# Attention's value products in three matmuls instead of two, with the fold of halves left out

## The reference

```python
p = jax.nn.softmax(logits.astype(jnp.float32), axis=-1).astype(v.dtype)
p_win = p[..., :n_keys_win].reshape(s_win.shape)
p_ctx = p[..., n_keys_win:]
return (jnp.einsum("bhqjrc,bqrjchd->bqjhd", p_win, vw)
        + jnp.einsum("bhqjn,bnhd->bqjhd", p_ctx, v_ctx))
```

## Time and profile before

| | us |
|---|---|
| median of 3 runs | 2239.29 |
| lowest, highest | 2235.98, 2240.27 |
| the profiled execution | 2240.01 |
| its span | 2237.8 |
| PE busy over the span | 2184.9 |
| DVE busy | 1654.8 |
| POOL busy | 1284.0 |
| ACT busy | 927.1 |
| attention's steps, first to last logits | 356.2 to 487.6 |

### The profile page before, as it was taken

One profiled execution on the slowest core, in us unless ns is written; L12 is line 12 of the kernel. 1 busy time (PEld: TensorE's weight loads), 2 busy tenths in 40 slices (PEclk: granted clock), 3 DMA queues, 4 the chain that ended last, 5 costly groups with the idle time before them and its releaser, 6 DMA issues.

```text
span 2237.8 us, 27901 instructions
## 1 busy us (share of the span) xinstructions
PE 2184.9 (98%) x10018; PEld 1778.9 (79%) x10018; DVE 1654.8 (74%) x1866; ACT 927.1 (41%) x1598; POOL 1284.0 (57%) x823
## 2 busy tenths in 40 slices
PE   8999998999999999999999999999999999999998
PEld 3788887887887887887888878888878788878886
DVE  5768773873688999987567797754879988877554
ACT  3555544871532232224446422234532233334443
POOL 3233312689776776667746455563476677657442
PEclk9999999999999999999999999999999999999999
DMA  9756657743436666659656233263245554567564
GB/s 334 234 135 177 172 164 194 174 139 116 154 126 209 214 221 237 230 179 311 196 189 202 93 112 105 95 226 118 67 162 197 188 180 163 188 238 234 192 188 151
DMA packets 359396, 403.09 MB, mean 180 GB/s; under 512 B 72063, under 2 KB 243291, under 8 KB 358363
## 3 DMA queue, kind: packets, MB, share of 16 engines
q1 hardware_dynamic: 321195, 377.70, 52.2%
q10 hardware_dynamic: 37488, 21.50, 3.4%
q0 software_dynamic: 576, 2.10, 0.2%
HBM read 293.47 MB, written 110.11 MB: 180 GB/s over the span
## 4 chain that ended last, share of the span: by engine, by line
PE 59%; POOL 14%; DMA 10%; DVE 10%; ACT 3%; issue 3%; SPq 1%; ACTq 0%; DVEq 0%; POOLq 0%
PE bank L1374 18%; PE bank L1376 17%; PE bank L1375 17%; POOL slot_lo L1274 5%; DMA pair_raw<-in_ffn_w_gu 5%; POOL slot L1274 5%; PE bank L1470 1%; POOL w_part L1294 1%; POOL w_part L1292 1%; PE bank L1611 1%; DMA q_spill<-qk_raw 1%; DVE t_sum L2472 1%; DVE pair_raw L2475 1%; DMA z_parts<-zt 1%; DVE t_sum L2467 1%
## 5 line engine op out<-in xcount | busy, mean ns | idle before, releaser
L1274 POOL TENSOR_TENSOR slot_lo<-pair_raw,slot_hi 128x512 fp32r<-128x512 f32 x106 | 188.6, 1782 | 278.3 <-ACT slot_hi L1918 278.3
L1274 POOL TENSOR_TENSOR slot<-pair_raw,slot 128x512 fp32r<-128x512 f32 x132 | 220.6, 1685 | 10.7 <-ACT slot L1918 10.7
L1918 ACT CAST slot_hi<-pair_raw 128x512 fp32r<-128x512 f32 x106 | 65.5, 618 | 361.4 <-DMA pair_raw<-in_ffn_w_gu 298.8
L1303 POOL TENSOR_TENSOR act_lo<-low_f,act_lo 128x512 fp32r<-128x512 f32 x96 | 139.1, 1461 | 109.1 <-ACT act_lo L1982 109.1
L1374 PE MATMUL bank<-a,slot_hi 128*128 128x512 f32 x460 | 183.0, 398 | 11.2 <-ACT zt L1943 8.0
L1376 PE MATMUL bank<-a,slot_hi 128*128 128x512 f32 x460 | 179.8, 391 | 0.0
L1375 PE MATMUL bank<-a,slot_lo 128*128 128x512 f32 x460 | 179.3, 390 | 0.0
L1274 POOL TENSOR_TENSOR slot_lo<-t_sum,slot_hi 128x512 fp32r<-128x512 f32 x103 | 155.3, 1528 | 38.0 <-ACT slot_hi L1918 38.0
L1374 PE MATMUL bank<-act_lo,slot_hi 128*128 128x512 f32 x412 | 160.6, 390 | 0.1
L1376 PE MATMUL bank<-act_lo,slot_hi 128*128 128x512 f32 x412 | 160.4, 389 | 0.0
L1375 PE MATMUL bank<-act_lo,slot_lo 128*128 128x512 f32 x412 | 160.3, 389 | 0.0
(11 more groups left out here) (372 smaller groups left out, 6350.5 us busy)
## 6 DMA issues: line engine op xcount, KB each, us to landing
pair_raw<-in_ffn_w_gu SPq DMA_DIRECT2D x80, 512.0 KB, 4.4
z_parts<-zt SPq DMA_DIRECT2D x148, 256.0 KB, 4.5
mod_in_f<-in_mod_w SPq DMA_DIRECT2D x48, 512.0 KB, 6.2
w_part<-in_ffn_w_down SPq DMA_DIRECT2D x88, 256.0 KB, 4.7
w_sums<-w_part SPq DMA_DIRECT2D x88, 256.0 KB, 5.1
low_f<-z_parts SPq DMA_DIRECT2D x88, 256.0 KB, 3.0
mod_in_p<-in_mod_w SPq DMA_DIRECT2D x32, 512.0 KB, 4.5
h_spill<-h SPq DMA_DIRECT2D x12, 1024.0 KB, 7.4
```

What stands on the lines that cost most here:

```text
L1274: nc.gpsimd.tensor_tensor(low, from_, high, ALU.subtract).then_inc(s_wlo, 1)
L1303: nc.gpsimd.tensor_tensor(lo, full, hi, ALU.subtract).then_inc(s_l2, 1)
L1918: nc.scalar.copy(slot(st, n, p)[0], from_).then_inc(s_whi, 1)
```

## The change

The values' high and low parts go into two tiles per pair of heads, `v_hi` and `v_lo`, each with the even head in columns 0 to 63 and the odd head in 64 to 127. A span of `values` is then a `product` of three matmuls. For an even head the stationary operand has columns 0 to 63 and the output rows 0 to 63; for an odd head it has all 128 columns and the output all 128 rows, of which only the upper 64 are read. The full sum stands in the head's own rows of bank 6. `low_part_moved` on ACT goes. DVE's `y_folded` becomes `y_scaled`: it multiplies bank 6 with the inverse rows into `y_f`, after waiting for the value products and the inverse rows. `inverse_rows` on ACT copies in the bank's order instead of regrouping. On POOL `y_ready` keeps the two operations of the split. The last block's separate product on DVE goes, and the wait for POOL (`s_preset` at 4) that stood before it moves to ACT.

```diff
-        v_st = [at(81, "v_even", [P, 2, TT + CT, P], F32R), at(91, "v_odd", [P, 2, TT + CT, P], F32R)]
+        v_hi, v_lo = at(81, "v_hi", [P, 2, TT + CT, P], F32R), at(91, "v_lo", [P, 2, TT + CT, P], F32R)
...
-                own, other = (slice(64 * a, 64 * a + 64) for a in (hh, 1 - hh))
+                own = slice(64 * hh, 64 * hh + 64)
                 one = ones[:, 0:64].rearrange("p (a c) -> p a c", a=1).to_broadcast([P, V_TILES, 64])
-                steps.run(nc.gpsimd.tensor_tensor(v_st[hh][:, slot, :, own], v_raw[:, :, own], one, ALU.mult))
-                nc.gpsimd.tensor_tensor(v_st[hh][:, slot, :, other], v_raw[:, :, own], v_st[hh][:, slot, :, own], ALU.subtract).then_inc(s_vp, 1)
+                steps.run(nc.gpsimd.tensor_tensor(v_hi[:, slot, :, own], v_raw[:, :, own], one, ALU.mult))
+                nc.gpsimd.tensor_tensor(v_lo[:, slot, :, own], v_raw[:, :, own], v_hi[:, slot, :, own], ALU.subtract).then_inc(s_vp, 1)
...
             def y_ready(g):
-                pool.wait_ge(s_fold, g + 1)
-                pool.wait_ge(s_invr, g + 1)
+                pool.wait_ge(s_yf, g + 1)
                 y, rows = block_of(g, y_f), rows_of(g)[0]
                 one_row = ones[rows, 0:32].rearrange("p (a c) -> p a c", a=1).to_broadcast([64, ROWS, 32])
-                nc.gpsimd.tensor_tensor(y, y, inv_rows[g % 2][rows, :].rearrange("p (r c) -> p r c", c=32), ALU.mult).then_inc(s_yf, 1)
-                pool.wait_ge(s_yf, g + 1)
...
                     if g:
-                        pe.wait_ge(s_fold, g)
+                        pe.wait_ge(s_yf, g)
                 for n in range(*PARTS[part]):
                     to, tile, i0, i1 = every[n]
-                    w, out_ = v_st[hd % 2][:, hd // 2 % 2, tile, :], bank[:, 6, i0 * P:i1 * P]
-                    pe.matmul(out_, w, pt_hi[buf][:, i0:i1, to, :], start=n == 0, stop=False)
-                    mm = pe.matmul(out_, w, pt_lo[buf][:, i0:i1, to, :], start=False, stop=n == len(every) - 1)
+                    rows = slice(0, 64 * (hd % 2 + 1))
+                    w, out_ = (v_hi[:, hd // 2 % 2, tile, rows], v_lo[:, hd // 2 % 2, tile, rows]), bank[rows, 6, i0 * P:i1 * P]
+                    mm = product(out_, w, pt_hi[buf][:, i0:i1, to, :], pt_lo[buf][:, i0:i1, to, :], n == 0, n == len(every) - 1)
...
-                nc.scalar.copy(inv_rows[g % 2][rows, :].rearrange("p (r j c) -> p j r c", j=4, c=COLS),
-                               bank[rows, 7, :].rearrange("p (j r c) -> p j r c", j=4, c=COLS)).then_inc(s_invr, 1)
-
-            def low_part_moved(g):
-                act.wait_ge(s_pv, g + 1)
-                nc.scalar.copy(block_tiles(g, y_f), bank[rows_of(g + 2)[0], 6, :].rearrange("p (j r c) -> p j r c", j=4, c=COLS)).then_inc(s_moved, 1)
+                nc.scalar.copy(inv_rows[g % 2][rows, :], bank[rows, 7, :]).then_inc(s_invr, 1)
...
-                if j >= 8 and j % 4 == 0 and j < STEPS + 8:
-                    low_part_moved(j // 4 - 2)
...
+            act.wait_ge(s_preset, 4)
             act.wait_ge(s_yf, BLOCKS)
             nc.scalar.copy(block_of(BLOCKS - 1, act_hi), block_of(BLOCKS - 1, y_f)).then_inc(s_yh, 1)
...
-            def y_folded(g):
-                y = block_tiles(g, y_f)
-                dve.wait_ge(s_moved, g + 1)
-                V.tensor_tensor(y, bank[rows_of(g)[0], 6, :].rearrange("p (j r c) -> p j r c", j=4, c=COLS), y, ALU.add).then_inc(s_fold, 1)
+            def y_scaled(g):
+                rows = rows_of(g)[0]
+                dve.wait_ge(s_pv, g + 1)
+                dve.wait_ge(s_invr, g + 1)
+                V.tensor_tensor(block_tiles(g, y_f), bank[rows, 6, :].rearrange("p (j r c) -> p j r c", j=4, c=COLS),
+                                inv_rows[g % 2][rows, :].rearrange("p (j r c) -> p j r c", j=4, c=COLS), ALU.mult).then_inc(s_yf, 1)
...
-            last_y, last_rows = block_of(BLOCKS - 1, y_f), rows_of(BLOCKS - 1)[0]
-            dve.wait_ge(s_preset, 4)
-            dve.wait_ge(s_fold, BLOCKS)
-            dve.wait_ge(s_invr, BLOCKS)
-            V.tensor_tensor(last_y, last_y, inv_rows[(BLOCKS - 1) % 2][last_rows, :].rearrange("p (r c) -> p r c", c=32), ALU.mult).then_inc(s_yf, 1)
             dve.wait_ge(s_yh, BLOCKS)
```

More of the change, by code:

```diff
@@ L287, in backbone @@
         s_pth, s_ptl = sem("turned_hi"), sem("turned_lo")
-        s_pv, s_moved, s_fold = sem("pv_done"), sem("y_low_part_moved"), sem("y_folded")
+        s_pv = sem("pv_done")
         s_yf, s_yh, s_yl = sem("y_scaled"), sem("y_hi"), sem("y_lo")
@@ L3021, in _ @@
                 if j >= 8 and j % 4 == 0:
-                    y_folded(j // 4 - 2)
-            last_y, last_rows = block_of(BLOCKS - 1, y_f), rows_of(BLOCKS - 1)[0]
-            dve.wait_ge(s_preset, 4)
-            dve.wait_ge(s_fold, BLOCKS)
-            dve.wait_ge(s_invr, BLOCKS)
-            V.tensor_tensor(last_y, last_y, inv_rows[(BLOCKS - 1) % 2][last_rows, :].rearrange("p (r c) -> p r c", c=32), ALU.mult).then_inc(s_yf, 1)
+                    y_scaled(j // 4 - 2)
             dve.wait_ge(s_yh, BLOCKS)
-            V.tensor_tensor(block_of(BLOCKS - 1, act_lo), last_y, block_of(BLOCKS - 1, act_hi), ALU.subtract).then_inc(s_yl, 1)
+            V.tensor_tensor(block_of(BLOCKS - 1, act_lo), block_of(BLOCKS - 1, y_f), block_of(BLOCKS - 1, act_hi), ALU.subtract).then_inc(s_yl, 1)
             for st in (F0, S, F1):
```

## The result

Over 13 runs each on one chip the changed kernel took 2245.78 us in the median (2240.77 to 2250.62), the kernel before 2236.97 (2233.99 to 2242.54). The ratio is 1.0039 [1.0031, 1.0047], that is +8.7 us, between 6.9 and 10.5. Slower was forecast, by 12.7; the sign was right and the size was 4 us too large. The time itself stands near the lower end of the stated range: 2245.78, where the range began at 2245 and the rival of the cheap narrow operand had 2244.4. The shift of 8.7 lies about halfway between the forecast's 12.7 and that rival's 5.1. So the time alone does not choose between them; the blocks do.

What follows compares the result with a forecast made beforehand. PE was taken to bound three of each attention block's four steps, DVE's loop the fourth. Blocks +15.2, disturbances -1.0, end -1.5 gave +12.7 us, 2252.0 against the median 2239.29; range 2245 to 2260, forecast 68%.

Steps and rivals of the forecast that it cites:

- the rival of the cheap narrow operand: Even heads' 64-wide matmuls cost half, savings run into DVE's loop: +5.1 us, 2244.4 us; chance 6%.
- The third matmul, 1.13 less 0.24 in a block: Attention blocks: one more matmul per span costs PE 1.13 us, filling 0.24 of waiting for DVE; net about 0.9.
- The widths, costed as equal: Even heads' value products: 64-column stationary operand priced like the 128-wide one, so no difference.
- The disturbances: Blocks 1 to 13: of 2.45 us of waits such as those behind ACT's LRU casts, 1.0 comes back.
- ACT's copy and POOL's products hidden: Attention stage: 16 ACT copies of 0.58 us and 15 POOL products of 1.29 bound no step.
- The add as a product at no cost: DVE's fourth step: product replaces add at the same place and size, 0.68 us, so zero change.
- Block 0, 1.5: First attention block: its 512-column products run at the lower clock, so the third matmul costs 1.5 us.
- The end, -1.5: End of attention: PE's waits for block 15's low part and the third output weight both go, -1.5 us.
- Late next is nothing that I can see: Behind the attention's end: no new wait, later stages are PE's and the shift is carried to the end.
- nothing is absorbed: Attention blocks: DVE's loop lengthens with PE's steps and POOL's lead does not help; 18.5 us, 2257.8; chance 12%.
- Faster: Attention steps: ACT, not PE, sets them, so the third matmul hides and the copies count; 2228.5 us; chance 4%.
- The drain: Even heads' value products: each width change drains the pipeline, 0.17 us each, 8 in all; 2260 us; chance 10%.

Runs made afterwards that it cites:

- third_only: Kernel before with the low-part product issued twice per span, copy, fold and POOL's products kept, 128-wide operand; ratio to before 1.0045.
- more_transposes: Changed kernel with two of the four transposes of the inverse sums issued twice in each block's step without value products; ratio to before 1.0046.
- two_of_three: Changed kernel without the product of the values' low part, so two matmuls per span; copy, fold and POOL's product stay removed; ratio to before 0.999.
- copy_back: Changed kernel with ACT's 16 copies of 0.58 us put back in their old place, DVE's product waiting for them; ratio to before 1.0043.
- all_wide: Changed kernel with all 128 columns as stationary operand for even heads too, waiting for both splits; ratio to before 1.0051.
- all_narrow: Changed kernel with a 64-wide stationary operand for odd heads too, written to rows 0 to 63 of the bank; ratio to before 1.0036.
- base_again: Kernel before, unchanged, run for a second profile; ratio to before 1.0004.
- casts_moved: Kernel before with the four LRU casts moved from ACT to POOL and block 14's product moved to DVE; ratio to before 0.9992.
- after_again: Changed kernel, unchanged, run for a second profile; ratio to before 1.0038.

## Why the prediction was right, and where it was not

The bound was read rightly. PE bounds three steps of four, the third matmul falls into these, and it costs its spacing and not its duration. The terms in their order:

- **The third matmul, 1.13 less 0.24 in a block: held, for the wide operand.** In third_only the blocks without a disturbance grew by 0.78 to 0.95. Its 13 blocks grew by 9.7, and as 1.7 of disturbance went in the same blocks, the undisturbed price is 11.4 / 13 = 0.88, for 0.89 predicted. The scores gave way after 0.59 instead of 0.83, and the fourth step stayed (more_transposes).
- **The widths, costed as equal: failed.** "I cost it as the 128-wide one, since what streams is the moving operand" holds for 512 and 384 columns and not for the small products, where by the reading above the load of the stationary operand sets the spacing, nor for the first product of a step. Seven even blocks less 0.16 each are the 1.1 us. Narrow was cheap indeed, but where that rival took 7.6 us off, the runs give 1.1: what is saved is at the 128-column products and at the first product of a group, not half of each product.
- **The disturbances, 1.0 back by "the copy gone and the steps longer": right in kind, wrong in cause and size.** 1.7 came back, all that the casts cost; the changed kernel loses 0.3 of it again in block 6. The length of the steps did it, and the copy has no part in it (third_only, two_of_three, copy_back). The prediction had both ends, 0 and 2.45; the upper one was too high, since it took an even head's block as the norm of all.
- **ACT's copy and POOL's products hidden: held** in the blocks (copy_back, and all_wide against third_only). The add as a product at no cost: held (0.67 for 0.68, and no wait on it up to block 13; for block 14, where the loop runs out, DVE waits 0.72 for the value products).
- **Block 0, 1.5: failed.** It was costed at the lower clock because the one execution at hand ran it there. At the full clock the difference is 0.2 to 0.5, and the level is the execution's.
- **The end, -1.5: two thirds right.** Both waits went, 1.46 us. "Late next is nothing that I can see" failed: PE waits for DVE's update of h, a gap of 0.38 (511.42 + 0.23 to 512.03). DVE can take the first output unit only when its last products are done, and the third writes the bank that this frees; as long as POOL's weight came later it did not show. The wait is the same 0.23 in all_wide, all_narrow, copy_back, more_transposes, two_of_three and third_only. In third_only, with POOL's load unchanged, the wait for POOL's weight is gone too, so it is PE's later arrival that removes that one; the wait for block 15's low part is 0.38 there and gone in all_wide, and block 15 is 0.6 us longer (10.82 for 10.23). The prediction did not see what the first wait was made of: in before DVE's low part of block 15 took 1.62 us where 0.69 is its usual time, because POOL's weight cast was running (see the last section). At 0.69 it would have been done at 505.18, before PE wanted it at 505.59.

Together: the sum was 12.7, and 11.2 of it from block 1 to unit 2, where the traces have 9.8 twice. Block 0's 0.2 makes 10.0 (10.3 if it is 0.5), within the 6.9 to 10.5 of the runs. The 2.7 between 12.7 and 10.0 are block 0's 1.3, the widths' 1.1 and the disturbances' 0.7, less 0.4 for the new wait at the end; what is smaller (block 6 below, block 14) is of the size of the rounding. The remaining 1.3 to the measured 8.7 is within the interval, and no run here tells whether it is more than chance; the stretch behind unit 2 alone differs by up to 5.4 us between profiles.

Of the rivals, *nothing is absorbed* fell by the filled 0.24 and the 1.7. *Faster* fell: ACT's 9.3 us of copies are worth 0.05. *The drain* fell as well. The rows of block 8 have a change of width in front of and behind each group of value products, and the even blocks came out shorter than the wide ones. The rule of the Trainium skill, TensorEngine Tiling (Array Packing), Tiling Modes, Key Properties, that a change of tiling mode drains the engine, is not seen at work here: from the transposes (442.60) to the narrow products is 0.35 us and in the wide block 0.36 (459.77 to 460.13), and the scores behind start 0.18 after the last narrow 384-column product, 0.17 behind a wide one. Whether a 64-wide operand counts as another mode is not told by the trace.

**Left open.** Block 6 (the second cast) is 0.33 longer than its like in after (9.16) and in every variant of it, and not in third_only. DVE's timeline shows the place:

```profile
425.26 0.82 DVE L2984 CUSTOM_DVE_ANT_0 probs<-bank,bias_t 128x640 f32<-128x640 f32 x1 [1.53 <-PE bank L1608]
```

The scores that it takes were written by about 424.95, and the releaser named is not theirs. The operation starts 0.78 us after the last product of its scores started. That distance is 0.78 in all seven profiles with the change, two_of_three included, and 0.55 at most in blocks 1 to 13 there at the other logits before which DVE sat idle for 0.2 us or more. As it stays the same however POOL's and the DMA's work falls beside it, it looks bound to this place of DVE's program, but what DVE waited for was not settled, and no run was made for it. Nor was a kernel run that relieves the end of before without moving work onto POOL.

## What to carry to other kernels

When a change trades matmuls for copies, ask which engine paces the step in which each stands: here 16 copies of 0.58 us and 15 POOL products of 1.29 were worth nothing in 13 blocks (all_wide against third_only) and about 0.6 us at the seam behind them, and 91 matmuls with spacings of 0.06 to 0.24 cost over eleven. Price a matmul by the spacing of starts at its own column count and its own stationary width; at 128 columns the load of the stationary operand seems to be the price. Where a wait at a seam goes, list every semaphore of the instruction that waited: the second latest is the new bound.

## What the runs showed of the hardware that was not expected

- A 64-column operand loads in 135 ns for 190, and products of 128 columns then follow 0.06 us apart for 0.11; at 512 columns the width makes no difference beyond the first product of a group (0.25 for 0.30).
- DVE's operations overlap their neighbours by about 0.08 to 0.1 us, except around one that writes rows 64 to 127, in before and after alike; it costs PE 0.13 us at every block of an odd head.
- One DVE operation, the same in both kernels (the low part of block 15, both inputs in SBUF), took 1.62 us in before and 0.69 in after. DVE's timeline of before has it, with after's row above:

```profile
504.49 1.62 DVE L3030 TENSOR_TENSOR act_lo<-y_f,act_hi 64x512 fp32r<-64x512 f32 x1 [0.69 <-ACT act_hi L2361]
```

  The times say that it waited for POOL within its printed duration. In before POOL's weight cast (503.27, 2.29 us) ends at 505.56, and the DVE operation ends 0.55 later. In all eight profiles in which it starts while a POOL operation has 0.3 us or more to go, it ends 0.54 to 0.55 after that operation, whatever it took: 1.62 in before, base_again and casts_moved, 2.12 in third_only, 2.87 in two_of_three, 1.94 in copy_back, 2.33 in more_transposes, 0.88 in all_narrow. In after, after_again and all_wide POOL's operation ended within 0.05 us of its start, and it took 0.69. POOL is held in its turn: the next cast of weights, which starts while this operation runs, takes 2.32 in after, where others of its form take 1.90. DVE's subtractions for pt_lo, which have one input in PSUM, show nothing of the kind: 57 of them between 375 and 500 us of after take 0.66 to 0.69 (512 columns) or 0.79 to 0.83 (640), and POOL is busy beside more than half of them. This is read from the times of eleven profiles; no run moved the cast away.
- The granted clock at the very start of the kernel was 0.76, 0.88 or 1.00 in executions that run the same code there, and the first scores came within a span of 3.9 us (351.4 to 355.3): nearly half of the effect measured here. A single pair of executions could not have shown it.
